# Sparse attention: two of the probability products move from GpSimd to VectorE, and TensorE takes the next head's scores ahead of the transposes

## The reference, cut to what matters

```python
n_cmp = (S - CMP_BLOCK) // CMP_STRIDE + 1          # 15
sc = einsum('bghqd,bgjd->bghqj', qb, kcmp) + head_bias(rel_c)
pc = masked_softmax(sc, rel_c >= 0) * (tpos >= CMP_BLOCK - 1)
oc = einsum('bghqj,bgjd->bghqd', pc, vcmp)
ps = masked_softmax(einsum('bghqd,bgqkd->bghqk', qb, kg) + bias_s, rel_s >= 0)
osel = einsum('bghqk,bgqkd->bghqd', ps, vg)
pw = masked_softmax(einsum('bghqd,bgkd->bghqk', qb, kwb) + head_bias(rel_w), mask_w)
ow = einsum('bghqk,bgkd->bghqd', pw, vwb)
return gb[:, 0, ..., None] * oc + gb[:, 1, ..., None] * osel + gb[:, 2, ..., None] * ow
```

## Time and profile before

| | |
|---|---|
| median of 3 runs | 2158.71 us (2158.61 to 2162.73) |
| the profiled execution | 2160.15 us |
| its span | 2158.4 us |
| mean granted PE clock | 0.92 of full |
| PE busy | 1731.5 us (80%) |
| DVE busy | 512.3 us (24%) |
| ACT busy | 435.4 us (20%) |
| POOL busy | 208.9 us (10%) |

### The profile page before, as it was taken

One profiled execution on the slowest core, in us unless ns is written; L12 is line 12 of the kernel. 1 busy time (PEld: TensorE's weight loads), 2 busy tenths in 40 slices (PEclk: granted clock), 3 DMA queues, 4 the chain that ended last, 5 costly groups with the idle time before them and its releaser, 6 DMA issues. The chain is left out here.

```text
span 2158.4 us, 30608 instructions
## 1 busy us (share of the span) xinstructions
PE 1731.5 (80%) x12608; PEld 1215.0 (56%) x12608; DVE 512.3 (24%) x804; ACT 435.4 (20%) x832; POOL 208.9 (10%) x198
## 2 busy tenths in 40 slices
PE   7999999888979999857675755799998675756756
PEld 6998489878468775523232322798756232322325
DVE  2643034444044432100000001444322000000004
ACT  3431033444033320000000002333401000000003
POOL 0013000122041010000000001411100000000002
PEclk9999999999999999799888888899998888988888
DMA  8458329324234524699999999444435999999993
GB/s 275 144 159 234 98 97 310 123 83 152 78 94 124 172 79 176 273 425 428 425 426 426 425 427 403 136 134 131 146 117 206 425 425 426 428 426 426 426 424 113
DMA packets 173164, 563.53 MB, mean 261 GB/s; under 512 B 12745, under 2 KB 127327, under 8 KB 140172
## 3 DMA queue, kind: packets, MB, share of 16 engines
q1 hardware_dynamic: 165168, 552.05, 66.6%
q10 hardware_dynamic: 7900, 10.13, 1.5%
HBM read 561.08 MB, written 5.23 MB: 262 GB/s over the span
## 5 line engine op out<-in xcount | busy, mean ns | idle before, releaser
L1274 PE MATMUL bank<-ring,big 128*32 128x256 f32 x4096 | 300.0, 446 | 201.0 <-DMA ring<-in_moe_w 201.0
L803 PE MATMUL bank<-big_r,ring_r 128*128 128x256 f32 (+1 forms) x2880 | 359.7, 286 | 2.7 <-DVE big_r L1633 1.4
L803 PEld LDWEIGHTS bank<-big_r,ring_r 128*128 128x128 f32 (+1 forms) x2880 | 351.2, 188 | 4.6 <-issue 4.3
L1274 PEld LDWEIGHTS bank<-ring,big 128*32 128x32 f32 x4096 | 157.3, 124 | 348.9 <-issue 304.0
L1645 DVE TENSOR_TENSOR ring_r<-ring,ring_r 128x2048 fp32r<-128x2048 f32 (+1 forms) x82 | 179.5, 2196 | 174.3 <-ACT ring_r L1353 173.9
L1371 ACT ACTIVATE big<-bank 128x512 f32<-128x512 f32 (+2 forms) x186 | 88.4, 490 | 575.3 <-PE bank L778 369.1
L1295 PE MATMUL bank<-ring,big 128*32 128x512 f32 x1024 | 137.9, 634 | 74.6 <-DMA ring<-in_moe_w 57.7
L778 PE MATMUL bank<-big 128*128 128x128 f32 (+5 forms) x634 | 113.9, 314 | 91.2 <-ACT big L1342 35.1
L1027 PE MATMUL bank<-ring,big 128*128 128x512 f32 (+1 forms) x416 | 179.8, 593 | 4.9 <-DVE big L1716 3.1
L803 PE MATMUL bank<-ring_r,big_r 128*128 128x256 f32 (+3 forms) x1440 | 180.8, 286 | 2.3 <-POOL ring_r L2052 2.3
L803 PEld LDWEIGHTS bank<-ring_r,big_r 128*128 128x128 f32 x1440 | 177.8, 198 | 4.2 <-DVE big_r L1633 3.1
(11 more groups left out here) (175 smaller groups left out, 1317.1 us busy)
## 6 DMA issues: line engine op xcount, KB each, us to landing
ring<-in_moe_w SPq DMA_DIRECT2D x128, 2048.0 KB, 23.6
ring<-in_moe_w SPq DMA_DIRECT2D x128, 1024.0 KB, 25.0
ring<-in_w_in SPq DMA_DIRECT2D x30, 1024.0 KB, 5.3
ring<-in_od_w_in SPq DMA_DIRECT2D x22, 1024.0 KB, 5.7
ring<-in_ev_w_in SPq DMA_DIRECT2D x11, 1024.0 KB, 11.4
ring<-in_ev_w_in SPq DMA_DIRECT2D x12, 768.0 KB, 4.6
ring<-in_od_cmp_w SPq DMA_DIRECT2D x8, 1024.0 KB, 8.9
ring<-in_od_w_out SPq DMA_DIRECT2D x8, 1024.0 KB, 6.1
```

What stands on the lines that cost most here:

```text
L803: ins = unit[0].mark(mm(dst, lhsT, rhs, start=start and n == 0, stop=stop and n == len(terms) - 1))
L1274: ins = mm(banks[5 + up][32 * j:32 * j + 32, 0:256], xg[:, k, q, :], wv[:, r, 256 * j:256 * (j + 1)], start=k == 0, stop=k == KC - 1)
```

## The change

DVE takes the tile 0 product and the compressed product from POOL and does them right behind `nfac`; a new semaphore, `n_early`, says that they are done. POOL keeps the tile 1 product alone and raises `n_probs` with it. In `nsa_T` PE waits for `n_early`, does the two transposes of tile 0, then waits for `n_probs` and does the rest. PE walks a list of its own, `ODD_PE`, in which the scores of head h+1 stand ahead of the transposes of head h for h = 0 to 10. The other engines keep their list.

```diff
+ODD_PE = list(ODD)
+for _h in range(NH - 1):
+    _k = ODD_PE.index(("NT", _h))
+    assert ODD_PE[_k + 1] == ("NS", _h + 1)
+    ODD_PE[_k:_k + 2] = [("NS", _h + 1), ("NT", _h)]
...
             def nsa_T(h):
 
-                pe.wait_ge(n_probs, h + 1)
+                pe.wait_ge(n_early, h + 1)
                 if h >= 1:
                     pe.wait_ge(n_pT, 3 * h)
-                for br in range(2):
-                    for t in range(TT):
+                for t in range(TT):
+                    if t == 1:
+                        pe.wait_ge(n_probs, h + 1)
+                    for br in range(2):
                         ins = tr(banks[5][:, br * T + t * P:br * T + (t + 1) * P], strided(
                             sx_at + (h % 2) * 2 * S_W + t * S_W + br * T, P, (1, P)))
...
-            for j, plan in enumerate((EVEN, ODD)):
+            for j, plan in enumerate((EVEN, ODD_PE)):
...
                              n_fac, h + 1)
+                        fac, p0 = nfac[:, h % 2], strided(base, P, (T, 2), (1, P))
+                        V.tensor_tensor(p0, p0, fac[:, 0, 1:3].unsqueeze(2).broadcast_to([P, 2, P]), ALU.mult)
+                        done(dve, V.tensor_tensor(cs_, cs_, fac[:, :, 0].unsqueeze(2).broadcast_to([P, 2, NCMP]), ALU.mult),
+                             n_early, h + 1)
...
-                        for t in range(TT):
-                            s_ = strided(base + t * S_W, P, (T, 2), (1, P * (t + 1)))
-                            g.tensor_tensor(s_, s_, fac[:, t, 1:3].unsqueeze(2).broadcast_to([P, 2, P * (t + 1)]), ALU.mult)
-                        s_ = strided(base + 2 * T, P, (S_W, 2), (1, NCMP))
-                        g.tensor_tensor(s_, s_, fac[:, :, 0].unsqueeze(2).broadcast_to([P, 2, NCMP]),
+                        s_ = strided(base + S_W, P, (T, 2), (1, T))
+                        g.tensor_tensor(s_, s_, fac[:, 1, 1:3].unsqueeze(2).broadcast_to([P, 2, T]),
                                         ALU.mult).then_inc(n_probs, 1)
```

More of the change, by code:

```diff
@@ L495, in build @@
             sem(n) for n in ("probs_ready", "pT_psum", "pT_ready", "pv_done", "pv_read"))
-        n_sc, n_read, n_max, n_exp, n_fac, n_probs, n_tp, n_pT, n_pv, n_y = (
-            sem("nsa_" + n) for n in ("scores", "scores_read", "max", "exp", "factor", "probs", "pT_psum", "pT", "pv", "y"))
+        n_sc, n_read, n_max, n_exp, n_fac, n_probs, n_early, n_tp, n_pT, n_pv, n_y = (
+            sem("nsa_" + n) for n in ("scores", "scores_read", "max", "exp", "factor", "probs", "probs_early", "pT_psum",
+                                      "pT", "pv", "y"))
         qkT_psum, qkT_ready = sem("qkT_psum"), sem("qkT_ready")
```

## The result

The changed kernel takes 2134.68 us (median of 4 runs, 2133.18 to 2137.30), the kernel before 2160.72 us beside it (4 runs, 2158.61 to 2162.88): a ratio of 0.9881, 95% interval 0.9863 to 0.9899, or 26.0 us less. The profiled execution has a span of 2134.3 us against 2158.4, 24.1 us less. A later set of runs of the same program gave 2133.61 us and a ratio of 0.9874 (0.9858 to 0.9891).

What follows compares the result with a forecast made beforehand. PE bound by waits for POOL's product and lower clock: 19.0 us idle, about 8 at lower clock, 1 of late starts, less 0.9, gain 26.8; 2158.7 - 26.8 = 2132 us, own range 2128 to 2136, with rivals 2126 to 2142.

Steps and rivals of the forecast that it cites:

- What bounds the kernel: Sparse-head part: engines wait in a circle, PE 19.0 us for POOL's last product, stretched by DVE's split; gaps lower PE's clock.
- POOL's product: POOL's remaining product takes 1.04 us, going first or behind both DVE products; probabilities ready 1.1 to 1.75 us behind the factor.
- DVE's products: Two new products a head, 0.42 + 0.20, 0.65 us with the start, fit DVE's 1.41 us idle gap before the split.
- PE's turn: PE's loop of transposes, projection, NV and scores takes 10.61 us a head and ends last, by a little.
- DVE's loop: Loop over DVE and ACT without PE: 10.82 or 10.09 us a head, 10.5 on average, just short of PE's.
- Head 10: With no projection, NV(10) directly behind the transposes waits for ACT's copies; 0.9 us lost.
- Further on: Behind the heads, the next part can take up the gain, since weight loads move with PE; clock drops may fall otherwise.
- Rival 3: Gain given back further on at a transfer not moving with PE; half gone 2145 us, all 2159; chance 0.05.
- rival 1: Loop over DVE and ACT ends last in the head part; 2134 us, or 2141 if the split waits; chance 0.07.
- Rival 2: PE's clock drops stay in the head turns, 1.65 us each; three give 2137 us, ten 2148; chance 0.12.

Runs made afterwards that it cites:

- e3: Kernel before, with POOL's small compressed product done first and its tile 1 product last, nothing else changed; 2140.85 us, ratio 0.9915.
- e4: Changed kernel with one more DVE instruction a head (a maximum over 1024 constant words, result unused) behind its two products; 2141.99 us, ratio 0.9920.
- e8: Kernel before, with POOL's small product first and PE's scores of head h+1 ahead of head h's transposes, all products on POOL; 2134.10 us, ratio 0.9870.
- e7: Changed kernel, but at head 10 PE's transposes stay ahead of the scores of head 11; 2134.26 us, ratio 0.9878.
- e1: Kernel before with only PE's order changed (scores ahead of transposes), all three products left on POOL; 2138.74 us, ratio 0.9903.
- e2: Changed kernel with PE's old order (transposes ahead of scores), so only the products are moved to DVE; 2137.48 us, ratio 0.9890.

## Why the prediction was right

**The forecast** of 2132 us lies 2.7 us below the measured 2134.68, which is inside the range of 2126 to 2142 and the forecast's own range of 2128 to 2136. Of the 2.7 us, 2.0 are the base: the forecast started from 2158.7, and the kernel before took 2160.72 beside the changed one. Against that the gain is 26.0 us, and 26.8 were forecast. That this is so close is in part luck, since two errors hide each other in it: the part gave 28.5 us, and in the profile 4.4 were lost further on.

**What bounds the kernel**: right. PE's waits for POOL are gone, the clock holds 1.00, and e3 shows the cause apart from the rest of the change.

**POOL's product**: it took 1.28 us in place of 1.04. It neither went first nor stood behind both DVE products: it was issued 0.04 us behind the first (445.72 and 445.76) and ahead of the second. At head 0 it was ready 1.36 us behind the factor and DVE's last product 1.40, within 1.1 to 1.75. That was just in time: DVE ended at 406.48 us, and PE began the transposes at 406.54.

**DVE's products**: 0.42 us for the first, as taken. The second was taken as 0.20 and took 1.03, since POOL's product had begun in between and DVE waited it out: POOL ended at 445.76 + 1.28 = 447.04 and DVE at 446.06 + 1.03 = 447.09. So they end 1.40 us behind the factor and not 0.65; this term was mis-sized by 0.75 us. The gap they lie in covered it with no room: at head 0 the products end at 406.48 us and ACT's high part (L1361) at 404.49 + 1.90 = 406.39, and the split starts 1.43 us behind the factor, where it was 1.41 before.

**PE's turn**: 10.61 us was taken from a turn of the kernel before, and 10.46 was measured. The transposes take 0.83 us of PE's time when the projection follows them (448.40 to 449.23) and 0.94 when the scores do; NV gives another 0.05. Ten turns make 1.5 us of the 1.7 by which the output product came earlier than forecast (515.03 against 516.7).

**DVE's loop**: 10.5 us forecast, 10.27 measured from factor to factor (10.68 and 9.86, alternating). It is indeed just short of PE's, as e4 and e8 show.

**Head 10**: 0.77 us lost, 0.9 forecast, and e7 takes it back.

**Further on**: the prediction took the lead as kept, and had only said that drops of the clock may fall otherwise. That term was mis-sized by 4.4 us in the profile. Rival 3 put such a loss down to a transfer; in the profile it was slower matmuls at a lower mean clock, in a stretch that the change doesn't touch. The medians put the loss at 2.5 us.

**The rivals**: rival 1 did not occur; e4 shows how little it would take: the two loops differ by 10.46 - 10.27 = 0.19 us a head. Rival 2 did not occur in the part, and e3 shows it alive: a gap of 1.99 us at head 0 was followed by transposes and scores at a mean granted clock of 0.60, 4.26 us long in place of 2.61, and a turn of 12.2 us. But a gap of 2.37 us at the same place in e1 left the clock at 1.00, as did 1.52 us in e2 and eight waits of 0.5 to 1.3 us in e4. So the length of the gap alone does not tell whether the level falls. The page "TensorE: Matmul & The Clock Gate" of the Trainium skill (section "A second HAM failure mode: psum-queue depth-cycling") is borne out by the earlier trace rows and this row of e3 as far as short idle stretches can cost the level; e1, e2 and e4 show that they need not:

```profile
404.60 1.33 PE L778 MATMUL bank<-big 128*128 128x128 f32 x8 [1.99 <-POOL big L2095]
405.73 1.06 PE L1158 MATMUL bank<-big 128*128 128x128 f32 x4
```

The stretches behind the gap in e3 and behind that in e1 (the granted clock is the third number from the right):

```profile
404.60:408.86 4.26, 4.26 (x20) 3.82 (x21) 2.09 (x1) 1.23 (x3) 0.00 (x0) 0.60 0.00 0
```

```profile
407.20:410.00 2.80, 2.80 (x25) 2.77 (x26) 2.33 (x6) 1.38 (x5) 0.00 (x0) 1.00 0.15 26
```

## What to carry to other kernels

Where two engines wait each other out, as GpSimd and VectorE do here, look at what the second one has queued when the long instruction of the first is due: reordering three products on GpSimd, at no cost, gave most of what the change gives. Where two loops run side by side and one is only a little shorter than the other, two remedies for the same wait don't add up, and the second should be judged by the margin it leaves. A gain in one stage may not reach the total in full. Where the same matmuls show a longer busy time at a lower granted clock and the idle time is as before, the loss is the clock and not a wait; one profiled execution does not tell whether the change brought it.

## What the runs showed of the hardware

- GpSimd and VectorE products with both inputs in SBUF wait each other out by whole instructions, in both directions: POOL's 0.24 us became 2.28 beside a split, DVE's small product took 1.03 us beside POOL's (by the nearest rows, 0.17 to 0.24 were to be expected), the split became 2.63 in place of 2.29, and POOL's 2 x 256 product 1.28 in place of 1.04. The Trainium skill ("GPSIMD Engine Reference", "Key points") states the contention, and the rows agree; that a product of 30 words can cost 2 us is what the rows add. The products of DVE with an input in PSUM showed none of it: L1677 lasted 0.69 us beside POOL's L2093 in the kernel before, and 0.68 in the changed kernel (as L1685) with POOL idle.
- The granted clock of PE differed between executions that do the same work. Between the two norms the same matmuls were busy for 231.9 to 237.8 us, and the stretch took 249.9 to 255.9 us in the lines above (256.6 in e7, of which 1.7 are more idle time and not the clock). Ahead of the part, where all eleven programs are the same, it took 396.6 to 403.9 us with 380.2 to 386.4 us of matmuls. Both are as large as the scatter of 3 to 9 us within one kernel's four runs.
